# Order of three short pieces of work around one weight unit in the second attention of a two-layer decoder trunk

## The reference, cut to what matters

```python
proj = h @ w_in                                    # queries, keys, values, indexer
_, idx = lax.top_k(score, n_sel)                   # per query, causal
s = einsum('bthgd,btkhd->bhgtk', q_blk, k_sel) * HEAD_DIM ** -0.5
pr = jax.nn.softmax(where(sel_ok, s, -inf), axis=-1)
out = einsum('bhgtk,btkhd->bthgd', pr, v_sel).reshape(B, S, QD)
x = x + rmsnorm(out @ w_out, g[1])
```

## Time and profile before

| | |
|---|---|
| median of three runs | 1077.97 us (1077.39 to 1078.35) |
| profiled execution | 1077.35 us, of which the span from its first to its last instruction is 1075.5 us |
| TensorE busy | 1055.0 us, 98% of the span |
| VectorE, ScalarE, GpSimd busy | 747.9, 538.1 and 192.8 us |
| mean granted clock of TensorE | 0.999 |
| HBM read | 96.88 MB, 92 GB/s over the span |

### The profile page before, as it was taken

One profiled execution on the slowest core, in us unless ns is written; L12 is line 12 of the kernel. 1 busy time (PEld: TensorE's weight loads), 2 busy tenths in 40 slices (PEclk: granted clock), 3 DMA queues, 4 the chain that ended last, 5 costly groups with the idle time before them and its releaser, 6 DMA issues.

```text
span 1075.5 us, 14866 instructions
## 1 busy us (share of the span) xinstructions
PE 1055.0 (98%) x5408; PEld 857.9 (80%) x5408; DVE 747.9 (70%) x1284; ACT 538.1 (50%) x1016; POOL 192.8 (18%) x335
## 2 busy tenths in 40 slices
PE   9999999999999999999999989999999999999997
PEld 8777779888888888888778766679888888888885
DVE  5455536586697696687579898536596696696684
ACT  6677545353453443425554567745254444453432
POOL 0465320000000000005403387520000000000005
PEclk9999999999999999999999999999999999999999
DMA  9531505644545445432613333006553535535502
GB/s 298 118 79 41 118 1 119 135 93 104 107 90 118 99 97 118 91 66 52 136 41 79 79 79 80 1 1 145 111 113 84 118 82 115 117 79 118 112 7 78
DMA packets 52009, 99.94 MB, mean 93 GB/s; under 512 B 4704, under 2 KB 4832, under 8 KB 51936
## 3 DMA queue, kind: packets, MB, share of 16 engines
q1 hardware_dynamic: 51216, 98.61, 41.0%
q10 hardware_dynamic: 720, 0.38, 0.1%
HBM read 96.88 MB, written 2.10 MB: 92 GB/s over the span
## 4 chain that ended last, share of the span: by engine, by line
PE 86%; DVE 7%; DMA 3%; ACT 1%; issue 1%; POOL 1%; SPq 1%; POOLq 0%; DVEq 0%; ACTq 0%
PE bank L2048 11%; PE bank L2049 11%; PE bank L2050 11%; PE bank L2413 7%; PE bank L2414 7%; PE bank L2415 7%; PE bank L2058 6%; PE bank L2060 5%; PE bank L2059 5%; PE bank L2439 3%; PE bank L2437 3%; PE bank L2203 3%; PE bank L2438 3%; PE bank L2272 2%; DMA w_raw<-in_a_w_in 2%; PE bank L2258 2%
## 5 line engine op out<-in xcount | busy, mean ns | idle before, releaser
L2048 PE MATMUL bank<-r_hi,w_hi 128*128 128x512 f32 (+1 forms) x456 | 177.5, 389 | 0.0
L2049 PE MATMUL bank<-r_hi,w_lo 128*128 128x512 f32 (+1 forms) x456 | 177.4, 389 | 0.0
L2050 PE MATMUL bank<-r_lo,w_hi 128*128 128x512 f32 (+1 forms) x456 | 177.4, 389 | 0.0
L1645 DVE TENSOR_TENSOR w_lo<-w_raw,w_hi 128x1024 fp32r<-128x1024 f32 x84 | 102.1, 1223 | 70.5 <-ACT w_hi L1174 70.4
L1174 ACT ACTIVATE w_hi<-w_raw 128x1024 fp32r<-128x1024 f32 x84 | 87.8, 1055 | 119.1 <-PE bank L2050 82.9
L2413 PE MATMUL bank<-w_hi,hid_hi 128*128 128x512 f32 x336 | 130.7, 389 | 0.0
L2414 PE MATMUL bank<-w_lo,hid_hi 128*128 128x512 f32 x336 | 130.7, 389 | 0.0
L2415 PE MATMUL bank<-w_hi,hid_lo 128*128 128x512 f32 x336 | 130.7, 389 | 0.0
L819 POOL TENSOR_TENSOR acc<-acc,G 128x512 f32<-128x512 f32 x8 | 13.0, 1652 | 594.3 <-ACT waste L1033 594.3
L1183 ACT ACTIVATE w_hi<-w_raw,gT 128x512 fp32r<-128x512 f32 x96 | 64.6, 716 | 107.0 <-DMA w_raw<-in_w_mlp_up 75.5
L2050 PEld LDWEIGHTS bank<-r_lo,w_hi 128*128 128x128 f32 (+1 forms) x456 | 85.2, 187 | 18.3
(11 more groups left out here) (213 smaller groups left out, 2148.7 us busy)
## 6 DMA issues: line engine op xcount, KB each, us to landing
w_raw<-in_w_mlp_up SPq DMA_DIRECT2D x64, 512.0 KB, 6.5
w_raw<-in_w_mlp_down SPq DMA_DIRECT2D x64, 512.0 KB, 6.9
w_raw<-in_b_w_in SPq DMA_DIRECT2D x16, 512.0 KB, 6.8
w_raw<-in_a_w_in SPq DMA_DIRECT2D x8, 512.0 KB, 8.9
w_raw<-in_a_w_out SPq DMA_DIRECT2D x8, 512.0 KB, 5.8
w_raw<-in_b_w_out SPq DMA_DIRECT2D x8, 512.0 KB, 6.1
xt<-in_x_turned SPq DMA_DIRECT2D x8, 256.0 KB, 5.2
X<-in_x SPq DMA_DIRECT2D x4, 512.0 KB, 11.2
```

Of the source, the lines that this page charges most:

```text
L1645: nc.vector.tensor_tensor(half_of(w_lo[:, u % 2, :], a), b_of(PRODUCTS[i][1], a), half_of(w_hi[:, u % 2, :], a).bitcast(f32), ALU.subtract ...
L2048: nc.tensor.matmul(bank, whi, xhi, start=start, stop=False)
L2049: nc.tensor.matmul(bank, wlo, xhi, start=False, stop=False)
L2050: return nc.tensor.matmul(bank, whi, xlo, start=False, stop=stop)
```

## The change

In VectorE's list, for layer 1 only, `o_low` now stands right behind `inverse` and ahead of the splits; this has an effect in turn 5 alone, where the order was `inverse(6)`, half of unit 61, `o_low(1)`, and is `inverse(6)`, `o_low(1)`, half of unit 61. In GpSimd's list `shared_split` is cut in two: the copy (`shared_high`) stays in turn 5, and the two subtractions (`shared_low`) go to turn 6, where they stand behind `normed(6)` and ahead of the first half of unit 62. No instruction is added or taken away.

```diff
-            def shared_split():
-
-                w_h, w_l = w_place(SHARED)
-                whole = raw(RAW[SHARED][0])
+            def shared_high():
+
+                w_h, whole = w_place(SHARED)[0], raw(RAW[SHARED][0])
                 pool.wait_ge(*loaded(SHARED))
                 pool.wait_ge(*w_spent(w_before(SHARED)))
                 nc.gpsimd.tensor_copy(w_h[:, 1024:2048], whole[:, 1024:2048]).then_inc(shared_hi, 1)
+
+            def shared_low():
+
+                w_h, w_l = w_place(SHARED)
+                whole = raw(RAW[SHARED][0])
                 pool.wait_ge(shared_hi, 1)
                 for k in (2, 3):
...
                     for u in SPLITS[layer].get(n - 2, ()):
-                        if u in POOL_UNITS and u != SHARED:
+                        if u == SHARED:
+                            shared_low()
+                        elif u in POOL_UNITS:
                             split_low(u, (2, 3))
                     for u in SPLITS[layer].get(n - 1, ()):
                         if u == SHARED:
-                            shared_split()
+                            shared_high()
                         elif u in POOL_UNITS:
                             split_low(u, (0, 1))
...
                     if layer and n + 1 < TURNS:
                         inverse(layer, n + 1)
+                    if layer and n >= 3 and n % 2:
+                        o_low(layer, (n - 3) // 2)
                     for u in SPLITS[layer].get(n - 1, ()) if n > 0 else ():
                         if u in NEXT_SLOT:
                             split(u)
...
-                    if n >= 3 and n % 2:
+                    if not layer and n >= 3 and n % 2:
                         o_low(layer, (n - 3) // 2)
```

## The result

The changed kernel takes 1082.59 us in the median of five runs (1081.36 to 1084.21), against 1077.97 us for the one before (1077.39 to 1078.49). The ratio is 1.0045, with a 95% interval of 1.0034 to 1.0056. The change makes it 0.45% slower, about 4.6 us. The forecast was 1080.4 us, with 1078.8 to 1083.2 as its range and C, a fall of TensorE's clock, as a rival at 1083.1.

The account below looks back on a forecast made before the run. The chain from unit 61's split through unit 63's load to turn 9's scores was taken as the bound; 2.45 us of lateness on 1077.35 gave 1079.8, plus 0.62 for the median: 1080.4 us, range 1078.8 to 1083.2.

Parts of the forecast that it names:

- C: TensorE's clock falls behind some 5 us idle ahead of turn 9's scores, costing 2.7 us: 1083.1 us; chance 0.15.
- Step 1: VectorE's o_low(1) ahead of its half of unit 61: TensorE's 1.98 us wait at turn 6 goes, gaining 1.9 us.
- Step 2: GpSimd's subtractions behind normed(6): it starts 0.26 us after the reciprocal; unit 61 split 1.36 us later without contention.
- Step 3: GpSimd and VectorE take turns, an instruction at a time; GpSimd's normed(6) loses 1.07 us to VectorE's half of unit 61.
- step 4: Along the chain, unit 63's load, turn 8's exponentials and turn 9's scores all come 2.45 us later.
- A: Rival: GpSimd loses nothing to contention during normed(6), unit 63's load is 1.36 us later: 1079.3 us; chance 0.14.
- B: Rival: unit 63's load lands sooner after issue and absorbs the lag; landing in 5.0 us gives 1078.55 us; chance 0.08.
- likeliest case: The forecast itself, unit 63's load 2.45 us later without a clock fall: 1080.4 us; chance 0.58.

Follow-up runs that it names:

- e5: Kernel before with one more wait on the load queue, holding the load of unit 63 until normed(6); 1083.39 us, ratio 1.0046.
- e6: Full change, but ScalarE does unit 63's high parts behind turn 8's exponentials, GpSimd all its low parts behind normed(8); 1077.13 us, ratio 0.9991.
- f7: e6 with the first half of TensorE's step of turn 3 moved to the end of turn 2; 1076.44 us, ratio 0.9978.
- e1: Kernel before with only the VectorE part of the change, GpSimd's order as before; 1078.76 us, ratio 1.0007.
- e3: Full change with VectorE's low part of its half of unit 61 made for 8 of 1024 columns; 1081.68 us, ratio 1.0030.
- f4: Full change with 18 more products in TensorE's gap ahead of the scores of turn 9; 1081.11 us, ratio 1.0023.
- e2: Kernel before with only the GpSimd part of the change, VectorE's order as before; 1082.04 us, ratio 1.0034.
- f6: Kernel before with 6 extra products at the end of TensorE's turn 2, ahead of turn 3's wait; 1078.30 us, ratio 1.0003.
- g2: Kernel before with only the first half of TensorE's step of turn 3 moved to the end of turn 2; 1078.32 us, ratio 0.9997.
- g1: f7 with VectorE's and GpSimd's order around unit 61 as in the kernel before; 1078.35 us, ratio 0.9995.

## Why the prediction was right in its direction, and what it missed

The reading of the bound was right: the wait at 637 in TensorE's list wasn't on the path, and the load of unit 63 was. e5 shows it without any other change, and e6 that it acts through the work on unit 63 that stood ahead of the exponentials.

Step 1, the gain of 1.9 us up to turn 7, came about in the full change but for a wait of 0.45 us, and it was worth nothing, as said. Its cause is the input of `o_low(1)`, `o_high(1)` on ScalarE: the text had its end 0.56 us ahead of the reciprocal of turn 6, and it came 0.29 us behind it (636.04 + 0.57 = 636.61). In f7, where the clock didn't fall in turn 3, it came 0.57 us ahead of it and no wait was left. Not said was that it needs the other half of the change at all: alone (e1) it stops at the turning of turn 6.

Step 2 holds: 0.26 us from the reciprocal to `normed(6)`, 2.54 us for the subtractions (2.53 used). Step 3, the loss by turns of 1.07 us, measured 0.98 (e3 against the full change), and `normed(6)` took 3.31 us in place of the 3.36 forecast. From the issue to the landing it took 650.07 - 642.42 = 7.65 us in place of 7.51. The sum of step 4, 2.45 us, is 2.52 from the rows and about 2.5 from f4's median. Rivals A and B are out: A by e3, B because the transfer took as long as before.

The median was outside the likeliest case's own range, 1079.6 to 1081.2, and 2.2 us above the 1080.4. The step that failed is not a term of the sum but the chance given to rival C, 0.15. Its condition, about 5 us of TensorE in one piece without work, was worked out in the same text (4.94 measured), and in all four profiles with a gap of 3.4 us or more the clock fell. I gave it a small chance because no row showed such a gap. What the Trainium skill (TensorE: Matmul & The Clock Gate, "Why this matters for your kernels") says on idle gaps spoke against the change, and these four profiles agree with it. C's price was 2.7 us, chosen as a third of an upper bound, so it is partly luck that it came near; it measured 2.07 in the rows, 2.4 in the medians of the full change and f4, and between 1.4 and 2.7 in e2, e3 and e5. The range of 8 in 10 held the result, 1082.59, only because it took in C at its middle price. With C as the forecast, the sum would have been 1077.97 + 2.45 + 2.7 = 1083.1, 0.5 us above the result.

What stays open: in what share of the executions the clock falls in turns 3 and 6 at waits under 2 us, and what it costs in the median. f6 and g2 removed one such wait, no gain can be measured, and g2's clock fell at the next one. The mean clocks on record bear on it: of the 91 executions of the kernel before that ran beside the experiments, 21 have 0.999, as its profile had, and against the medians of their own series these are 0.7 us below the others. A mean doesn't say where the clock fell, so this is an estimate of what the falls cost together. How much of f7's gain over g1 is the work and how much such falls isn't settled either, as g1's profile has a fall in this stretch.

## What to carry to other kernels

Before an engine's wait is removed, ask whether the chain that ended last goes through it; if it doesn't, the time comes back as a longer wait further on. A subtraction, a copy or a rounding that frees a buffer is really the start of a transfer, and moving it behind other work moves the transfer and all that stands in order behind its first use. When a forecast sum leaves TensorE one long gap, price the lower clock behind it as a term of the sum. And what a reordering is worth depends on the wait that ends last: the same edit that cost 0.45% here is part of the fastest kernel, at 0.9978 of the time before, once the exponentials no longer stand behind unit 63; that kernel without the edit is at 0.9995.

## What the runs showed of the hardware that was not expected

TensorE's granted clock fell in the middle of the kernel, behind gaps of 4.94, 4.54, 4.24 and 3.41 us, and matmuls of 128x512 went from 0.39 to 0.63 us. With the full change it wasn't restored at the first product but some 4 us later. It fell also, in eight of ten profiles, around a wait of 1.69 us, and the two executions without the fall had the same wait. Behind the wait of turn 6, 1.97 to 1.99 us, it fell in f5 and g1 and not in the kernel before, e5 and f6. At such places one execution shows the fall and the next doesn't, and nothing here says why.

A GpSimd operation and a VectorE one with two inputs in SBUF take turns: the normalising took 3.31 and 3.22 us with a VectorE subtraction of 1024 columns beside it, and 2.33 without. The Trainium skill (SBUF — State Buffer, "SBUF: two separate sides") describes this as a lock held for a whole instruction, and these durations agree with it.
